# Context rows of the pooling layer normed while the down projection runs, and the layer's first panel read for context rows first

## The chip, the core and the metric

The kernel runs on one core of a Trainium2 chip. Five engines work side by side and meet only in semaphores: TensorE (PE, with its weight loads as PEld), VectorE (DVE), ScalarE (ACT), GpSimd (POOL) and SyncE (SP), which issues most of the DMAs. The metric is the device time of one execution in microseconds, the median of several runs; lower is better.

## The reference, cut to what matters

The program is two transformer blocks in a row on 256 tokens ("latent" rows) of width 2048. The first ends in a gated feed-forward layer; the second starts with a pooling layer that works on the latent rows and, apart from them, on 256 "context" rows with weights in common. Both sets of rows are normed, scaled and shifted before the pooling layer's input projection:

```python
x = x + jnp.einsum('bsf,fd->bsd', jax.nn.silu(gate) * up, w_down[l])      # 5632 -> 2048
...
shift, scale, gate = jnp.split(jax.nn.silu(c) @ ada_w[i] + ada_b[i], 3, axis=-1)
h_lat = rms_norm(x, pre_norm[i]) * (1 + scale[:, None]) + shift[:, None]
shift_c, scale_c, gate_c = jnp.split(jax.nn.silu(c_ctx) @ ada_w[i] + ada_b[i], 3, axis=-1)
h_ctx = rms_norm(ctx, pre_norm[i]) * (1 + scale_c) + shift_c
# pool_branch(h), for h_lat and h_ctx:
u, gate = jnp.split(h @ w_in, 2, axis=-1)
p = centred_multiscale_pool(u.reshape(B, L, POOL_GROUPS, POOL_GROUP_DIM))
```

h_lat needs x after the last column of the down projection. h_ctx needs nothing of the first block: only the input ctx, and the vectors shift and scale (the "ada" products), which the kernel computes on VectorE along the way.

## The kernel before, in words

**Weights as a stream of chunks.** All weight matrices pass through one ring of four slots (RING). A chunk is 256 rows by 512 columns, 512 KB. SP loads it into `raw`; ACT rounds it to `hi` (L541); DVE writes `lo` = raw - hi (L545); PE multiplies with both, three products for each (L598, `by_tokens`), since the fp32 values are carried as a high and a low part. SP may load the next chunk into a slot when `lo` of the old one is written (`lo_split`); ACT may overwrite `hi` when PE has used the old one (`chunks_used`). Between the weight chunks come chunks of the ada matrix, which PE does not see: DVE multiplies them with a vector in four instructions (L574). The order of both kinds is a list written out in advance (`DOWN_ORDER`, `POOL_ORDER`), and each engine has its own program in which the calls `his`, `los` and `by_tokens` walk through that list; whatever else stands between two calls runs at that place of its engine and holds back what is behind it.

**The down projection.** Four panels of 512 output columns, 22 weight chunks each, in two turns (i = 0 and 1) of two panels. In a turn the weight chunks are called w0 to w43 here; w22 is the first of the second panel. Twelve matmuls (2 of rows by 2 of tokens by 3) make a chunk. Eight ada chunks (a0 to a7, a8 to a15) lie among the chunks of each panel; in the second half the stream reads w31 w32 a12 w33 w34 a13 w35 w36 w37 a14 w38 w39 a15 w40 w41 w42 w43. After each panel DVE adds the sums in PSUM to the residual (`add_panel`, L1621) and ACT squares the new columns (`panel_squares`, L682).

**From there to the pooling layer.** `n_pool` is one norm over four token tiles, in two parts: context rows first, then latent rows. The context part is done near the end of turn 1: ACT squares its rows (L673), DVE forms the mean (L749), POOL the root (L754), DVE scales the rows (L759). The latent part follows the last `add_panel`. When both are scaled PE turns the rows to columns (transposes, L775) in 16 groups of four, four groups ahead of the first chunk and four more ahead of each of the next three; ACT applies scale and shift from PSUM to `shift_tmp` (L805), DVE writes `h_hi` (L830) and `h_lo` (L837) out of it. Four banks of PSUM hold the turned groups, so group g waits for `h_lo` of group g - 4. Each chunk of the first pooling panel (L598 again, 24 matmuls, four token tiles) waits for the norm's groups that it reads. The averaging matrix `poolm` (1 MB), first read at L2202, is loaded by a DMA that ACT issues (L1299) after the last `add_panel`, and PE waits for it ahead of the transposes. The tiles `h4_hi` and `h4_lo` lie over the tiles `g_hi` and `g_lo`, which the down projection reads to its last chunk.

## Time and profile before

| | us |
|---|---|
| median of 3 runs | 2441.76 |
| lowest and highest | 2439.11 and 2446.45 |
| the profiled execution's own time | 2439.29 |
| its span in the trace | 2437.5 |
| mean granted TensorE clock | 0.987 of full |

```profile
PE 2336.4 (96%) x11221; PEld 1935.8 (79%) x11221; DVE 1656.9 (68%) x2401; ACT 1041.2 (43%) x1490; POOL 76.2 (3%) x112
PE   8999999999999999999969999999999699899997
PEclk9999999999999999999989999999999899999999
```

The first line gives each engine's busy time, its share of the span and its instructions. The other two cut the span into 40 slices of 61 us, each digit a tenth: how busy PE was, and which share of full speed its clock was granted. PE is the engine that is busy nearly all the time, save in a few slices; the digit 6 in the 21st slice (1219 to 1280 us) is the passage from the down projection to the pooling layer.

### The profile page before, as it was taken

The numbers are of one execution on the slowest core, as the hardware profiler recorded it, in microseconds if no ns is written. First come the engines' busy times: TensorE is split into PE (matmuls) and PEld (weight loads), VectorE is DVE, ScalarE is ACT, GpSimd is POOL, SyncE is SP. The second block draws the span as 40 slices with busy tenths as digits, with TensorE's granted clock in tenths as the row PEclk, the third lists the DMA queues.
The fourth block names the chain that finished last, engine by engine and source line by source line (L and its number), as shares of the span: only waits on it lengthen the run. The fifth ranks groups of instructions, "written<-read, shape, count | busy, mean of one in ns | idle before, by whom it ended". The sixth has DMA issues, their size and how long they took to land.

```text
span 2437.5 us, 32050 instructions
## 1 busy us (share of the span) xinstructions
PE 2336.4 (96%) x11221; PEld 1935.8 (79%) x11221; DVE 1656.9 (68%) x2401; ACT 1041.2 (43%) x1490; POOL 76.2 (3%) x112
## 2 busy tenths in 40 slices
PE   8999999999999999999969999999999699899997
PEld 6778778878877877778858888887788699799976
DVE  5378866687787786777748585756758666456544
ACT  5575654555555555333342222222222535443433
POOL 1022210000000000000000000000000000000000
PEclk9999999999999999999989999999999899999999
DMA  7956545666676766777735464645557256312243
GB/s 240 206 167 197 165 137 158 189 217 219 209 234 199 232 212 201 249 238 243 249 108 185 144 198 137 200 139 171 205 169 221 82 170 181 114 61 68 74 140 136
DMA packets 225516, 430.32 MB, mean 177 GB/s; under 512 B 13800, under 2 KB 38624, under 8 KB 224129
## 3 DMA queue, kind: packets, MB, share of 16 engines
q1 hardware_dynamic: 222112, 418.96, 55.2%
q10 hardware_dynamic: 2720, 9.83, 1.3%
q8 instruction: 63, 1.03, 0.2%
q14 instruction: 45, 0.36, 0.1%
q0 software_dynamic: 576, 0.14, 0.0%
HBM read 426.16 MB, written 2.72 MB: 176 GB/s over the span
## 4 chain that ended last, share of the span: by engine, by line
PE 63%; issue 19%; DVE 7%; DMA 6%; ACT 4%; DVEq 0%; POOL 0%; ACTq 0%; SPq 0%; POOLq 0%
PE ps L598 37%; PE ps L631 11%; PE ps L608 9%; DMA raw<-in_w_down 4%; DVE lo L545 2%; ACT hi L541 2%; DVE ada_acc L574 2%; PE ps L647 1%; DVE ustage L1630 1%; DMA raw<-in_w_in 1%; PE ps L2202 1%; PE ps L2127 0%; DMA poolm<-const_pool 0%; PE ps L1979 0%; PE ps L775 0%
## 5 line engine op out<-in xcount | busy, mean ns | idle before, releaser
L541 ACT ACTIVATE hi<-raw 128x1024 fp32r<-128x1024 f32 x604 | 635.3, 1059 | 1148.8 <-PE ps L598 536.2
L545 DVE TENSOR_TENSOR lo<-raw,hi 128x1024 fp32r<-128x1024 f32 x604 | 731.4, 1222 | 520.4 <-ACT hi L541 517.5
L574 DVE SCALAR_TENSOR_TENSOR ada_acc<-raw,csil,ada_acc 128x512 f32<-128x512 f32 x720 | 491.8, 746 | 2.5 <-DMA raw<-in_ada_w 2.3
L598 PE MATMUL ps<-hi,h_hi 128*128 128x512 f32 x960 | 383.2, 399 | 8.1 <-DVE lo L545 6.5
L598 PE MATMUL ps<-hi,h_lo 128*128 128x512 f32 x960 | 378.9, 395 | 0.0
L598 PE MATMUL ps<-lo,h_hi 128*128 128x512 f32 x960 | 378.7, 395 | 0.0
L598 PEld LDWEIGHTS ps<-hi,h_hi 128*128 128x128 f32 x960 | 180.8, 188 | 55.4 <-DVE lo L545 13.4
L598 PEld LDWEIGHTS ps<-hi,h_lo 128*128 128x128 f32 x960 | 180.7, 188 | 42.5
L598 PEld LDWEIGHTS ps<-lo,h_hi 128*128 128x128 f32 x960 | 180.9, 188 | 40.1
L598 PE MATMUL ps<-hi,g_hi 128*128 128x512 f32 x352 | 140.9, 400 | 6.6 <-DVE lo L545 6.3
L631 PE MATMUL ps<-hi,h_hi 128*128 128x512 f32 (+1 forms) x352 | 142.2, 404 | 2.9 <-DVE h_lo L736 2.9
L598 PE MATMUL ps<-lo,g_hi 128*128 128x512 f32 x352 | 139.1, 395 | 0.0
L598 PE MATMUL ps<-hi,g_lo 128*128 128x512 f32 x352 | 139.0, 395 | 0.0
L631 PE MATMUL ps<-hi,h_lo 128*128 128x512 f32 (+1 forms) x352 | 136.9, 389 | 0.0
L631 PE MATMUL ps<-lo,h_hi 128*128 128x512 f32 (+1 forms) x352 | 136.6, 388 | 0.0
L598 PE MATMUL ps<-hi,k_hi 128*128 128x448 f32 (+2 forms) x288 | 102.6, 356 | 1.1 <-DVE k_lo L837 0.6
L598 PE MATMUL ps<-hi,y_hi 128*128 128x512 f32 x256 | 102.6, 401 | 0.0
L608 PE MATMUL ps<-h_hi,hi 128*128 128x512 f32 x256 | 102.0, 398 | 0.0
L598 PE MATMUL ps<-hi,y_lo 128*128 128x512 f32 x256 | 101.9, 398 | 0.0
L598 PE MATMUL ps<-lo,y_hi 128*128 128x512 f32 x256 | 101.9, 398 | 0.0
L598 PE MATMUL ps<-hi,k_lo 128*128 128x448 f32 (+2 forms) x288 | 101.5, 353 | 0.0
L598 PE MATMUL ps<-lo,k_hi 128*128 128x448 f32 (+2 forms) x288 | 101.5, 352 | 0.0
(320 smaller groups left out, 3710.3 us busy)
## 6 DMA issues: line engine op xcount, KB each, us to landing
raw<-in_ada_w SPq DMA_DIRECT2D x192, 512.0 KB, 4.2
raw<-in_w_up SPq DMA_DIRECT2D x176, 512.0 KB, 4.5
raw<-in_w_down SPq DMA_DIRECT2D x88, 512.0 KB, 5.4
raw<-in_w_in SPq DMA_DIRECT2D x84, 512.0 KB, 4.5
raw<-in_pool_w_in SPq DMA_DIRECT2D x64, 512.0 KB, 4.1
raw<-in_mla_w_in SPq DMA_DIRECT2D x56, 448.0 KB, 4.1
raw<-in_w_out SPq DMA_DIRECT2D x32, 512.0 KB, 3.8
raw<-in_pool_w_out SPq DMA_DIRECT2D x32, 512.0 KB, 4.7
```

What stands on the lines that cost most here:

```text
L541: act.activation(hi[:, slot, :, :], raw[:, slot, :, :], ACT.Copy).then_inc(hi_split, 1 + ada)
L545: dve.tensor_tensor(lo[:, slot, :, :], raw[:, slot, :, :], hi[:, slot, :, :].bitcast(F32), ALU.subtract).then_inc(lo_split, 1)
L574: ins = dve.scalar_tensor_tensor(acc, raw[:, slot, k, :], csil[:, v, kt:kt + 1], acc, ALU.mult, ALU.add)
L598: mm = pe.matmul(ps[:, bank, 0:n], a[:, kt0 + k, tok * P:(tok + 1) * P], w[:, slot, k, col0:col0 + n], start=first and k == 0 and s == 0, ...
L608: mm = pe.matmul(ps[:, bank0 + n, :], w[:, slot, k, n * P:(n + 1) * P], a[:, kt0 + k, :], start=first and k == 0 and s == 0, stop=last and ...
L631: mm = pe.matmul(ps[:, PAIR * half + tok, 0:width], x, w[:, k, :], start=first and k == 0 and s == 0, stop=last and k == nk - 1 and s == 2)
L647: mm = pe.matmul(ps[:, bank, at:at + 1], acc, negones[:, 0:1], start=True, stop=True)
L1630: ins = dve.scalar_tensor_tensor(conv[which][:, m, back:SEQ], turned_u(m)[:, 0:SEQ - back], cols[:, bass.ds(ch + vec[0] * P + vec[1], 1)], ...
L2202: mm = pe.matmul(ps[:, m, s * SEQ + c0:(s + 1) * SEQ], u[:, TT * s + k, m * P:(m + 1) * P], poolm[:, bass.ds(n, 1), k, c0:].rearrange("p a ...
```

## The change

Nine edits, all around that passage.

1. `n_pool` is split in two norms of two token tiles, `n_pool_ctx` and `n_pool` (latent), of eight groups each; a group is still four transposes. `g_hi` and `g_lo` become halves of one tile that interleaves them, so that both free the same low addresses as the down projection goes on, and `h4_hi` and `h4_lo` of the context rows can be written while it runs.
2. The context rows are squared (ACT), their mean formed and the rows scaled (DVE) in turn 0 of the down projection, between its chunks.
3. In the second panel of turn 1, ahead of each of the chunks w31 to w38, PE makes one group of context transposes (`ctx_turn`, into banks 4 and 7 by turns); ACT writes both the shifted rows and `h_hi` from PSUM, four activations for a group (`ctx_high`); DVE writes `h_lo` (`ctx_low`).
4. The two panels of a turn swap their banks of PSUM, so that the last one leaves the banks of the context tiles free.
5. The scales and shifts are made (`scales`) at the start of turn 1.
6. The DMA of `poolm` is issued in turn 0, and PE waits for it only at its first use.
7. At the end DVE adds the last panel ahead of the third of the next stage's `lo` instead of behind it.
8. PE's loop over the two turns is written out.
9. The first pooling panel (`first_pool_panel`) takes its first four chunks for the context tiles, then the same four, which are kept in the ring (`frees=False`), for the latent tiles, then the last four for both.

```diff
+CTX_FROM = FT // CK_T + CH + 1
...
-        g_hi = pl("g_hi", [P, FT, SEQ], F32R)
-        g_lo = pl("g_lo", [P, FT, SEQ], F32R)
+        g = pl("g", [P, FT, 2, SEQ], F32R)
+        g_hi, g_lo = g[:, :, 0, :], g[:, :, 1, :]
...
+        def ctx_turn(pe, g):
+            n = n_pool_ctx
+            if g == 0:
+                pe.wait_ge(n.scaled, n.scaled0 + n.nt)
+            else:
+                pe.wait_ge(n.hi_done, n.groups0 + max(g - 1, 0))
...
+        def ctx_high(act, g):
+            n = n_pool_ctx
+            act.wait_ge(n.turned, n.groups0 + g + 1)
...
+            for to, done in (((lambda m: n.tmp[:, g % SHIFT_BUFS, m * SEQ:(m + 1) * SEQ]), n.shifted),
+                             ((lambda m: n.hi[:, g * n.per + m, :]), n.hi_done)):
+                for m in range(n.per):
...
+        def ctx_low(dve, g):
+            n = n_pool_ctx
+            dve.wait_ge(n.shifted, n.groups_shifted0 + g + 1)
+            dve.wait_ge(n.hi_done, n.groups0 + g + 1)
+            dve.tensor_tensor(n.lo[:, g * n.per:(g + 1) * n.per, :],
...
         @block.scalar
-                if i == D // W // 2 - 1:
-                    norm_squares(act, n_pool, lambda e, i: e.wait_ge(ctx_loaded, 16), 0, xn4[:, 0, :])
+                if last:
+                    act.wait_ge(scales_ready, 2)
+                    for g in range(n_pool_ctx.groups):
+                        end = place(DOWN_ORDER, CTX_FROM + g) + RING
+                        his(act, C_DOWN, i, step, at, end)
+                        ctx_high(act, g)
+                        at = end
+                else:
+                    act.wait_ge(g_lo_done, FREE + N_UP)
+                    act.dma_start(poolm[:, :, :, :], consts["pool"]).then_inc(poolm_loaded, 16)
+                    end = place(DOWN_ORDER, CTX_FROM) + RING
+                    his(act, C_DOWN, i, step, at, end)
+                    norm_squares(act, n_pool_ctx, lambda e, i: e.wait_ge(ctx_loaded, 16), 0, xn4[:, 0, :])
...
         @block.tensor
-            pe.wait_ge(poolm_loaded, 16)
+            def first_pool_panel():
+                part = lambda s, j, frees: by_tokens(pe, C_POOL + j, (C_POOL + j) % RING, h4_hi, h4_lo, CK_T * j, streams[s * TT:(s + 1) * TT],
+                                                     W, j == 0, False, ada_behind(C_POOL + j), frees)
+                pe.wait_ge(ffn_added, PAIR + D // W - 1)
+                pe.wait_ge(n_pool_ctx.lo_done, n_pool_ctx.all_groups)
+                for j in range(RING):
+                    if j == RING - 1:
+                        pe.wait_ge(ffn_added, PAIR + D // W)
+                        pe.wait_ge(ada_taken, FREE + ADA_POOL)
+                        norm_turn(pe, n_pool, 0, TURN_BANKS)
+                    part(CTX, j, False)
+                for j in range(RING):
+                    if j:
+                        norm_turn(pe, n_pool, TURN_BANKS + 2 * (j - 1), min(TURN_BANKS + 2 * j, n_pool.groups))
+                    pe.wait_ge(n_pool.lo_done, n_pool.groups0 + j + 1)
+                    part(LAT, j, True)
```

The instruction streams show three places. First ACT in the second panel of turn 1, around chunk w34 (`hi` is the weight chunk's high part, `xn` the norm's rows, `h_hi` the normed columns). Before:

```order
L541 ACTIVATE hi<-raw 128x1024 [waits chunks_used,raw_loaded0]
L541 ACTIVATE hi<-raw 128x1024 [waits chunks_used,raw_loaded2]
L541 ACTIVATE hi<-raw 128x1024 [waits chunks_used,raw_loaded3]
L541 ACTIVATE hi<-raw 128x1024 [waits chunks_used,raw_loaded1]
L541 ACTIVATE hi<-raw 128x1024 [waits chunks_used,raw_loaded2]
```

The second, third and fourth of these in the changed kernel:

```order
L543 ACTIVATE hi<-raw 128x1024 [waits chunks_used,raw_loaded2]
L815 ACTIVATE ctx_tmp<-ps,adat,hscale 128x256 [waits norm_turned]
L815 ACTIVATE ctx_tmp<-ps,adat,hscale 128x256
L815 ACTIVATE h_hi<-ps,adat,hscale 128x256 x2
L543 ACTIVATE hi<-raw 128x1024 [waits chunks_used,raw_loaded3]
L815 ACTIVATE ctx_tmp<-ps,adat,hscale 128x256 [waits norm_turned]
L815 ACTIVATE ctx_tmp<-ps,adat,hscale 128x256
L815 ACTIVATE h_hi<-ps,adat,hscale 128x256 x2
L543 ACTIVATE hi<-raw 128x1024 [waits chunks_used,raw_loaded1]
```

Four activations now stand between one chunk's `hi` and the next, eight times over. The second place is DVE at the end of the down projection. Before:

```order
L749 TENSOR_SCALAR ms<-ss 128x2 [waits norm_squared]
L759 TENSOR_SCALAR xn_112<-xn_112,rstd 128x2048 [waits norm_root]
L759 TENSOR_SCALAR xn_112<-xn_112,rstd 128x2048
L545 TENSOR_TENSOR lo<-raw,hi 128x1024 [waits hi_split] x3
L653 TENSOR_SCALAR adat<-ps 128x8 [waits ada_turned]
L1621 TENSOR_TENSOR xres<-ps,xres 128x2x512 [waits chunks_used]
```

And now:

```order
L824 TENSOR_TENSOR h_lo<-ctx_tmp,h_hi 128x2x256 [waits norm_hi_done,norm_shifted]
L547 TENSOR_TENSOR lo<-raw,hi 128x1024 [waits hi_split] x5
L656 TENSOR_SCALAR adat<-ps 128x8 [waits ada_turned]
L1674 TENSOR_TENSOR xres<-ps,xres 128x2x512 [waits chunks_used]
L547 TENSOR_TENSOR lo<-raw,hi 128x1024 [waits hi_split]
L748 TENSOR_REDUCE ss<-panel_sums 128x2 [waits x_squared]
```

The context norm is gone from ahead of the last addition to the residual, and one `lo` has moved behind it. The third place is the same norm on DVE where it has gone, turn 0 of the down projection, between the chunks w36 and w37:

```order
L576 SCALAR_TENSOR_TENSOR ada_acc<-raw,csil,ada_acc 128x512 [waits ada_added] x2
L547 TENSOR_TENSOR lo<-raw,hi 128x1024 [waits hi_split] x2
L752 TENSOR_SCALAR ms<-ss 128x2 [waits norm_squared]
L762 TENSOR_SCALAR xn_111<-xn_111,rstd 128x2048 [waits norm_root]
L762 TENSOR_SCALAR xn_111<-xn_111,rstd 128x2048
L547 TENSOR_TENSOR lo<-raw,hi 128x1024 [waits hi_split]
```

What stood here before was three `lo` in a row, behind the same ada chunk.

## Rows read from the trace of the kernel before

**Rows 1.** Windows: length, busy us (count) of PE, PEld, DVE, ACT, POOL; clock, DMA share, GB/s.
```profile
1172.00:1235.00 63.00, 61.66 (x280) 49.60 (x278) 45.88 (x53) 28.37 (x31) 0.69 (x1) 1.00 0.75 238
1235.00:1253.70 18.70, 3.68 (x17) 3.28 (x17) 10.76 (x19) 6.12 (x13) 0.70 (x1) 0.63 0.49 168
```

**Rows 2.** Waits, 985 to 1262 us: who waited for whom, us, times, longest.
```profile
ACT hi L541 <- DMA raw<-in_w_down: 127.4, 67, 5.4
PE ps L775 <- DMA poolm<-const_pool: 13.7, 1, 13.7
PE ps L598 <- DVE lo L545: 6.3, 10, 0.9
```

**Rows 3.** Timeline of PE, end of down projection to pooling panel: start, us, what, [idle].
```profile
1231.73 0.48 PE L598 MATMUL ps<-hi,g_hi 128*128 128x512 f32 x1
...
1234.38 0.40 PE L598 MATMUL ps<-hi,g_lo 128*128 128x512 f32 x1
1248.50 3.68 PE L775 MATMUL ps<-ident,xn 128*128 128x128 f32 x16 [13.73 <-DMA poolm<-const_pool]
1253.70 0.51 PE L598 MATMUL ps<-hi,h_hi 128*128 128x512 f32 x1 [1.52 <-DVE h_lo L837]
...
1259.38 1.47 PE L775 MATMUL ps<-ident,xn 128*128 128x128 f32 x12
...
1262.56 0.48 PE L598 MATMUL ps<-hi,h_hi 128*128 128x512 f32 x1
...
1308.35 0.40 PE L608 MATMUL ps<-h_hi,hi 128*128 128x512 f32 x1
```

**Rows 4.** Timeline of DVE in the same stretch.
```profile
1231.90 2.48 DVE L759 TENSOR_SCALAR xn<-xn,rstd 128x2048 f32<-128x2048 f32 x2 [0.81 <-POOL rstd L754]
1234.30 3.49 DVE L545 TENSOR_TENSOR lo<-raw,hi 128x1024 fp32r<-128x1024 f32 x3
...
1237.78 1.22 DVE L1621 TENSOR_TENSOR xres<-ps,xres 128x1024 f32<-128x1024 f32 x1
...
1241.71 2.48 DVE L759 TENSOR_SCALAR xn<-xres,rstd 128x2048 f32<-128x2048 f32 x2 [0.81 <-POOL rstd L754]
...
1261.41 0.68 DVE L837 TENSOR_TENSOR h_lo<-shift_tmp,h_hi 128x512 fp32r<-128x512 f32 x1
1262.01 0.42 DVE L830 CAST h_hi<-shift_tmp 128x512 fp32r<-128x512 f32 x1
```

**Rows 5.** Timeline of ACT in the same stretch.
```profile
1226.81 1.90 ACT L673 ACTIVATE xn<-xn 128x2048 f32<-128x2048 f32 x1
...
1230.80 2.94 ACT L541 ACTIVATE hi<-raw 128x1024 fp32r<-128x1024 f32 x3
...
1260.02 3.85 ACT L805 ACTIVATE shift_tmp<-ps,adat,hscale 128x256 f32<-128x256 f32 x8 [6.55 <-PE ps L775]
```

**Rows 6.** DMA issues, 975 to 1000 us: count, size, us to landing.
```profile
raw<-in_ada_w SPq DMA_DIRECT2D x3, 512.0 KB, 6.1
```

**Rows 7.** DMA issues, 985 to 1236 us.
```profile
raw<-in_ada_w SPq DMA_DIRECT2D x30, 512.0 KB, 4.8
```

**Rows 8.** Timelines of ACT, DVE and PE in turn 0, chunks w33 to w37.
```profile
1071.40 1.06 ACT L541 ACTIVATE hi<-raw 128x1024 fp32r<-128x1024 f32 x1 [0.31 <-DMA raw<-in_w_down]
...
1080.46 1.06 ACT L541 ACTIVATE hi<-raw 128x1024 fp32r<-128x1024 f32 x1 [0.27 <-DMA raw<-in_w_down]
1071.12 2.59 DVE L545 TENSOR_TENSOR lo<-raw,hi 128x1024 fp32r<-128x1024 f32 x2 [0.44 <-ACT hi L541]
1073.63 2.73 DVE L574 SCALAR_TENSOR_TENSOR ada_acc<-raw,csil,ada_acc 128x512 f32<-128x512 f32 x4
...
1078.88 0.50 PE L598 MATMUL ps<-hi,g_hi 128*128 128x512 f32 x1 [0.62 <-DVE lo L545]
```

**Rows 9.** Groups by line, 1193.5 to 1226 us: count, busy us, mean ns, idle before.
```profile
L545 DVE TENSOR_TENSOR lo<-raw,hi 128x1024 fp32r<-128x1024 f32 x12 | 14.7, 1225 | 6.8 <-ACT hi L541 6.6
L541 ACT ACTIVATE hi<-raw 128x1024 fp32r<-128x1024 f32 x12 | 12.7, 1061 | 21.6 <-DMA raw<-in_w_down 21.6
```

More of the change, by code:

```diff
@@ L589, in los, with by_tokens @@
                     split_lo(dve, i * step + c, c % RING)
-        def by_tokens(pe, c, slot, a_hi, a_lo, kt0, outs, width, first, last, ada=0):
+        def by_tokens(pe, c, slot, a_hi, a_lo, kt0, outs, width, first, last, ada=0, frees=True):
             pe.wait_ge(lo_split, c + RING + 1)
@@ L599, in by_tokens @@
                                        start=first and k == 0 and s == 0, stop=last and k == CK_T - 1 and s == 2)
-            mm.then_inc(chunks_used, 1 + ada)
+            if frees:
+                mm.then_inc(chunks_used, 1 + ada)
         def by_channels(pe, c, slot, a_hi, a_lo, kt0, bank0, first, last, ada=0):
@@ L787, in norm_ahead @@
                 pe.wait_ge(n.lo_done, n.groups0 + -(-(j + 1) * CK_T // n.per))
+        def ctx_turn(pe, g):
[5 more added lines that the diff above has]
+            for m in range(n.per):
+                for i in range(n.nt):
+                    mm = pe.transpose(ps[:, 4 + 3 * (g % 2), (m * n.nt + i) * P:(m * n.nt + i + 1) * P],
+                                      n.xn(i)[:, (g * n.per + m) * P:(g * n.per + m + 1) * P], ident)
+            mm.then_inc(n.turned, 1)
+        def ctx_high(act, g):
+            n = n_pool_ctx
+            act.wait_ge(n.turned, n.groups0 + g + 1)
+            if g >= SHIFT_BUFS:
+                act.wait_ge(n.lo_done, n.groups0 + g - SHIFT_BUFS + 1)
+            for to, done in (((lambda m: n.tmp[:, g % SHIFT_BUFS, m * SEQ:(m + 1) * SEQ]), n.shifted),
+                             ((lambda m: n.hi[:, g * n.per + m, :]), n.hi_done)):
+                for m in range(n.per):
+                    k = g * n.per + m
+                    ins = act.activation(to(m), ps[:, 4 + 3 * (g % 2), m * SEQ:(m + 1) * SEQ], ACT.Identity,
+                                         scale=n.scale(k, 0), bias=n.shift(k, 0))
+                ins.then_inc(done, 1)
+        def ctx_low(dve, g):
[3 more added lines that the diff above has]
+            dve.tensor_tensor(n.lo[:, g * n.per:(g + 1) * n.per, :],
+                              n.tmp[:, g % SHIFT_BUFS, :].rearrange("p (m n) -> p m n", m=n.per),
+                              n.hi[:, g * n.per:(g + 1) * n.per, :].bitcast(F32), ALU.subtract).then_inc(n.lo_done, 1)
         def norm_parts(n, g):
@@ L1080, in _ @@
             x_power(pool, 1)
-            for part in range(2):
-                norm_root(pool, n_pool, part)
+            norm_root(pool, n_pool_ctx)
+            norm_root(pool, n_pool)
             def yout_roots(m):
@@ L1620, in add_panel @@
                 v = xres[:, :, bass.ds(col0, W)]
-                dve.tensor_tensor(v, ps[:, 2 * half:2 * half + 2, :], v, ALU.add).then_inc(done, 1)
+                dve.tensor_tensor(v, ps[:, 2 - 2 * half:4 - 2 * half, :], v, ALU.add).then_inc(done, 1)
             def older_taps(i, which):
@@ L1723, in yout_join @@
                    .then_inc(yout_added[m], 1)
-            scales(0, V_PRE0)
-            norm_mean(dve, n_pool, 1)
-            norm_apply(dve, n_pool, 1)
+            n = FT // CK_T
+            for i in range(D // W // 2):
+                order, step, last = DOWN_ORDER, len(DOWN_ORDER), i == D // W // 2 - 1
+                mid = place(order, DOWN_TURN) + 1 + RING
+                end = place(order, n) + RING
+                split = lambda a, b: los(dve, C_DOWN, i, step, a, b, ADA_DOWN, 2)
+                if last:
+                    scales(0, V_PRE0)
+                split(RING, end)
+                add_panel(ffn_added, i * step + used(C_DOWN + end - RING), 0, i * 2 * W)
+                split(end, mid)
+                take_ada(dve, i * 2 + ADA_DOWN, 5)
+                at = mid
+                if last:
+                    for g in range(n_pool_ctx.groups):
+                        to = place(order, CTX_FROM + g) + RING
+                        split(at, to)
+                        ctx_low(dve, g)
+                        at = to
+                else:
+                    to = place(order, CTX_FROM + 3) + RING
+                    split(at, to)
+                    norm_mean(dve, n_pool_ctx)
+                    norm_apply(dve, n_pool_ctx)
+                    at = to
+                split(at, step)
+                los(dve, C_DOWN, i, step, step, step + RING - 1 - int(last))
+                take_ada(dve, i * 2 + ADA_DOWN + 1, 5)
+                add_panel(ffn_added, i * step + used(C_DOWN + step), 1, i * 2 * W + W)
+                los(dve, C_DOWN, i, step, step + RING - 1 - int(last), step + RING - int(last))
+            norm_mean(dve, n_pool)
+            norm_apply(dve, n_pool)
+            los(dve, C_DOWN, D // W // 2 - 1, step, step + RING - 1, step + RING)
             norm_shift_split(dve, n_pool)
@@ L2164, in _ @@
             n = FT // CK_T
-            with pe.Fori(0, D // W // 2) as i:
+            for i in range(D // W // 2):
                 def ada_before(j):
+                    if i == D // W // 2 - 1 and 0 <= j - CTX_FROM < n_pool_ctx.groups:
+                        ctx_turn(pe, j - CTX_FROM)
                     if j < n and j * CK_T % 4 == 0:
```

56 lines of the change are left out of this document (26 added, 30 removed).

## The prediction

> **What bounds the kernel now.** I read the windows first, then the waits, then the timelines of the engines in two stretches. In the windows the reader is to see a down projection in which PE is busy 61.7 of 63.0 us, and then 18.7 us in which it is busy 3.7, on a clock granted at 0.63, between its two levels of 1.2 and 2.4 GHz [rows 1]. The waits name two things. In the passage, PE stands 13.7 us for the DMA of `poolm`. In the down projection ACT stands 127.4 us for weight chunks still being loaded, and PE ten times, 6.3 us together, for `lo` [rows 2]. So PE is the bound there by a small margin, and the ring behind it (load, `hi`, `lo`, free the slot, load again) is nearly as slow: little can be put into ACT or DVE without PE seeing it.
>
> **The passage, before.** The last down chunk, w43, starts on PE at 1231.73 and its last matmul at 1234.38; the first pooling panel starts at 1253.70, and the instruction behind that panel (L608) at 1308.35 [rows 3]. From the start of w43 to L608: 76.62 us. In it, 24 matmuls of a pooling chunk take 5.58 us at the steady pace (0.2325 us each; 1253.70 to 1259.38 with the start), eight chunks 44.64 us, and w43 2.79 us. The remaining 29.2 us are a gap of 19.2 us (1234.5 to 1253.70) and three breaks of about 3.3 us: from the transposes at 1259.38 to the next matmul at 1262.56 it is 3.18 us [rows 3]. The gap has layers. DVE adds the last columns at 1237.78, though PE was done 3 us before, since the context norm and three `lo` stood ahead; the latent rows are scaled at 1244.2 [rows 4]; then only `poolm` is missing, until 1248.5. So `poolm` alone is worth 4.3 us, not the 13.7 of its row.
>
> **The passage, after.** Call T the time at which w43 is done. At T PE can go on with context tiles, 12 matmuls or 2.79 us for each of four chunks. Meanwhile the chain to the latent rows runs: from the start of the addition to scaled rows it takes 1237.78 to 1244.19, 6.4 us, with work between that is now elsewhere [rows 4]. It is done at T+6.7, and PE asks for it ahead of the fourth chunk, at T+8.4: 1.7 us to spare. There it makes 16 transposes. Twelve take 1.47 us in a row, 0.102 each without the tail [rows 3], so 16 and the restart of the matmuls take 1.72 us. ACT starts 0.64 us after the first group (1260.02 against 1259.38) and needs 0.48 us for an activation, 0.96 for a group [rows 3, 5]; on DVE a group takes a cast and a subtraction, 0.94 us (0.60 from subtraction to cast, 0.34 for the cast) [rows 4]. With the cast of group 1 ahead of `h_lo` of group 0, that `h_lo` is done at T+12.1. PE ends the fourth context chunk at 8.4 + 1.7 + 2.8 = T+12.9. The latent halves follow at T+12.9, 16.6, 20.3 and 23.1, with eight transposes (0.91 us) ahead of the second and third; each finds its group ready. The next chunk's `hi` waits on ACT for the last of the eight groups (T+22.0), its `lo` is done at T+24.9, and PE wants it at T+25.9. Behind it stand two ada chunks (4.9 us), then the next `lo` at T+30.8, wanted at T+31.4. The margins are 1.7, 0.8, 1.0 and 0.6 us, and I count no wait. From w43's start to L608: 2.79 + 44.64 + 1.72 + 2 x 0.91 = 51.0 us. **Saved: 76.6 - 51.0 = 25.6 us.** If the margins fail one after another, up to 4 us of it go.
>
> **Turn 0 pays for the context norm.** ACT's squares take from 1226.81 to 1230.80, 4.0 us [rows 5]. They now stand ahead of `hi` of w34, which starts at 1071.40 right behind its load [rows 8]: it starts at 1075.0 instead, its `lo` is done at 1077.4 instead of 1073.7, and PE, which took w34 at 1075.3, takes it 2.1 us late. The ada chunk behind (2.65 us) then pushes `lo` of w35 to 1081.2 against 1078.88, when PE took it with no slack [rows 8]: 2.3 us late. DVE's part, 0.17 + 0.81 idle for POOL + 2.48 [rows 4], ends at 1085.8; w37, whose load is later too (it was split at 1080.46 [rows 8], and its slot frees 3.7 us late), is done at 1087.0: 2.4 us late, so this part is nearly hidden. But the ada chunks and `lo` of w38 to w40 stand behind it, and their slots free 3.5 to 4.3 us late: PE takes w38 3.5 us late and w40 4.2 us. After that PE was ahead of the ring no longer than its own pace allows, and nothing is caught up. **+4.2 us.** Bounds: 2 us (later slack takes some back) and 4.0 + 3.5 = 7.5 us, both blocks in full.
>
> The DMA of `poolm` lands in the ring's busiest stretch. The trace has a like case: while the 2 MB of context rows were loaded, ada chunks took 6.1 us to land, against 4.8 in the whole stage [rows 6, 7]: 1.3 us. For 1 MB and a ring of which every load counts I take **+1 us**, between 0 and 3. The Trainium skill, "DMA: Bandwidth & Descriptors", section "Issuing engines are not separate DMA queues", says that transfers issued by different engines share the same 16 DMA engines and interleave, so ACT's queue gives no way round the ring. By that rule all of 1 MB would come out of the ring's bandwidth, an estimate of 3 us at the 238 GB/s and 0.75 busy of [rows 1], and the sum would be 2 us worse; the trace's 1.3 us for twice the bytes speaks for less.
>
> **Turn 1 pays for the context groups.** Eight times four transposes cost PE 0.41 us and 0.09 at the restart, 4.0 us in all, and give the ring that much more time. ACT gets 8 x 1.93 us. It was idle 21.6 us over 12 `hi` in this stretch, 1.8 each, and DVE 6.8 us [rows 9]. `ctx_low` is 0.60 us [rows 4], in the time in which DVE waits for `hi` anyway. Walking through w33 to w43 as above, with three ada chunks between: `lo` of w35 at 1208.6 for PE at 1208.55, w38 at 1217.5 for 1218.5, w40 at 1224.2 for 1224.1, w41 at 1227.0 for 1227.0. So ACT and DVE are just full, PE just not held up, and the two short waits that it had before here (0.56 and 0.55 us, among the ten) are swallowed. w43 starts 2.6 us later than before. **+2.6 us.** This is an operation of which the trace has no copy: ACT writes the rounded high part straight from PSUM with scale and bias. Its nearest row is the 0.48 us of L805 [rows 5]. Bounds: 1 us, and 4.0 + 8 x (1.93 - 1.8 / 2) = 12 us if half the idle time of ACT is not where it is wanted.
>
> The rest I take at nothing: PE's loop written out (w43 of turn 0 to w0 of turn 1 was 2.88 us from start to start, 0.09 over the pace), the scales in turn 1 (0.5 us on DVE, where PE was 3 to 4 us behind the ring), the swap of banks, the interleaved tile (the same elements for each instruction).
>
> **The sum.** -25.6 + 4.2 + 1.0 + 2.6 = -17.8 us. Against the profiled execution's 2439.3 us it is 2421.5; that execution lay 2.5 us under the median of the runs, which would give 2424. I forecast 2423.
>
> **The rivals.**
> *The ring pays little* (chance 0.12). What is late in turn 0 is caught up, `poolm` is free: costs 3 us instead of 7.8, 2418. For it: PE was 3 to 4 us behind the ring at the end of turn 0. Against: that slack is used up by w4 of turn 1, and the ring is late by as much.
> *The panel's start is not ready* (0.10). The four margins of 0.6 to 1.7 us fail, or the first pooling chunks' `lo`, now behind the eight `ctx_low`, come late: 5 us back, 2428. Against: the raw chunks are there, and only two `lo` are left ahead of T.
> *The ring pays about double* (0.15). The two walks assume that landing times move only by what their slots are late. If each ACT block falls where a load has just landed, turn 1 costs 8 and turn 0 7.5 with 2 for the DMA: 17.5 against 25.6, 2433.
> *The ring pays for everything: slower* (0.05). One mechanism: a ring of four slots bound by latency has no free time, and each microsecond given to ACT or DVE in it returns on PE. Price: turn 0 4.0 + 3.5 + 3, turn 1 8 x (1.93 + 0.60) = 20.2: 30.7 us, 5 more than the passage gives, 2446. It decides once the insertions cost over 25.6 us. For it: ACT's 127.4 us of waits are all for loads. Against: they are idle time of ACT, 1.8 us each, which the insertions fill.
> *The change doesn't do what it says* (0.03): a wait serialises context tiles and norm as before, and only the 7 us of `poolm` and the late addition are won against 7.8 paid: no change, 2441.
>
> **How the numbers follow.** My forecast has 0.55. Differences under 0.3%, 7 us, can't be told from no change. Faster by more: the forecast, the cheap ring, the late start and most of the double price, 0.88. Within: the rest of the double price and the last rival, 0.07. Slower 0.05. The forecast's own range is 2418 to 2428; with the neighbours to both sides 2414 to 2433, which leaves the slower cases and a part of the double price out.
>
> **What would show it.** Right: L608 starts about 51 us after w43; no idle PE over 2 us between w43 and L608, and a granted clock of 1.00 there; w43 of turn 1 starts 6 to 10 us later than 1231.73; in turn 1 PE waits for `lo` within w31 to w43 sum to under 2 us; `poolm` is no releaser of PE. Wrong: idle time of PE ahead of the transposes or between the latent halves (the start); PE's waits for `lo` in the two second halves over 15 us (the ring).

## The result: 2420.05 us, a ratio of 0.992

The changed kernel took 2420.05 us (median of 4 runs, 2417.38 to 2424.76) against 2440.44 us of the kernel before on the same chip: ratio 0.992, 95% interval 0.9899 to 0.9941. A second comparison gave 2418.37 against 2437.94 us, 0.992 (0.9906 to 0.9933). The forecast was 2423.

The profiled execution took 2424.76 us, its span is 2423.0 us. From its page:

```profile
PE 2336.9 (96%) x11221; PEld 1935.5 (80%) x11221; DVE 1652.8 (68%) x2393; ACT 1048.0 (43%) x1506; POOL 75.1 (3%) x112
PE   8999999999999999999999999998999699899997
PEclk9999999999999999999999999999999899899999
```

TensorE does the same work in the same busy time; its digit 6 in the 21st slice has become a 9. Where the 14.5 us between the two spans are, by the starts of the same matmuls on TensorE (w0 of turn 0, w0 of turn 1, w43 of turn 1, L608, which is L611 here):

| | before | after | difference |
|---|---|---|---|
| to w0 of turn 0 | 971.58 | 977.95 | +6.37 |
| turn 0 | 135.04 | 137.35 | +2.31 |
| turn 1 to w43 | 125.11 | 127.86 | +2.75 |
| passage, w43 to L608 | 76.62 | 51.01 | -25.61 |
| from there to the end | 1129.14 | 1128.78 | -0.36 |

Nothing was put into or taken out of the first row; only the layout of `g_hi` and `g_lo`, which are written there, is new. In the thirteen other executions profiled for this document it lies between 968.8 and 976.0 us, with a mean of 973.0 us over the three kernels with the old layout and 972.8 us over the eleven executions with the new one: it is scatter, and it hides 6 us of the gain in this pair of profiles, though not in the medians.

**The passage.** Windows of the changed kernel (columns as in [rows 1]), its waits (994 to 1270 us), and TensorE's timeline, which answer to [rows 1 to 3]:

```profile
1181.00:1243.16 62.16, 61.94 (x299) 50.22 (x298) 49.63 (x59) 38.48 (x58) 0.00 (x0) 1.00 0.74 244
1243.16:1265.00 21.84, 21.84 (x109) 18.14 (x109) 11.37 (x19) 8.09 (x17) 0.70 (x1) 1.00 0.24 75
```

```profile
ACT hi L543 <- DMA raw<-in_w_down: 108.7, 52, 5.9
...
PE ps L600 <- DVE lo L547: 6.9, 9, 1.9
```

```profile
1243.16 0.48 PE L600 MATMUL ps<-hi,g 128*128 128x512 f32 x1
...
1246.04 0.39 PE L600 MATMUL ps<-hi,h_hi 128*128 128x512 f32 x1
...
1254.41 1.91 PE L778 MATMUL ps<-ident,xn 128*128 128x128 f32 x16
1256.07 0.48 PE L600 MATMUL ps<-hi,h_hi 128*128 128x512 f32 x1
...
1261.73 1.03 PE L778 MATMUL ps<-ident,xn 128*128 128x128 f32 x8
...
1265.40 1.03 PE L778 MATMUL ps<-ident,xn 128*128 128x128 f32 x8
...
1271.85 0.39 PE L600 MATMUL ps<-hi,h_hi 128*128 128x512 f32 x1
...
1277.43 0.40 PE L600 MATMUL ps<-hi,h_hi 128*128 128x512 f32 x1
...
1294.17 0.40 PE L611 MATMUL ps<-h_hi,hi 128*128 128x512 f32 x1
```

Where there were 13.7 and 1.5 us of idle time [rows 3], no row has a bracket: TensorE is busy 21.84 of 21.84 us, at a clock of 1.00 instead of 0.63. The context matmuls (`h_hi` at 1246.04) begin 0.23 us behind the last one of w43, the pace of any two matmuls. With T = 1245.95 (w43's start and 2.79) the transposes are at T+8.46 and the fourth context chunk at T+10.12. The latent halves follow at T+13.0, 16.6, 20.2 and 23.1, the second and third behind eight transposes each (1261.73 and 1265.40); the fifth chunk, for all four tiles, is at T+25.9 (1271.85), the sixth at T+31.5 (1277.43), and L611 is 51.01 us behind the start of w43. `poolm` releases nobody.

The latent chain beside it, on DVE and ACT, for [rows 4, 5]:

```profile
1246.24 1.23 DVE L1674 TENSOR_TENSOR xres<-ps,xres 128x1024 f32<-128x1024 f32 x1 [2.74 <-PE ps L600]
...
1250.19 2.48 DVE L762 TENSOR_SCALAR xn<-xres,rstd 128x2048 f32<-128x2048 f32 x2 [0.81 <-POOL rstd L757]
```

```profile
1257.35 0.68 DVE L876 TENSOR_TENSOR h_lo<-shift_tmp,h_hi 128x512 fp32r<-128x512 f32 x1
...
1269.57 1.22 DVE L547 TENSOR_TENSOR lo<-raw,hi 128x1024 fp32r<-128x1024 f32 x1
...
1275.48 1.22 DVE L547 TENSOR_TENSOR lo<-raw,hi 128x1024 fp32r<-128x1024 f32 x1
```

```profile
1255.04 3.76 ACT L844 ACTIVATE shift_tmp<-ps,adat,hscale 128x256 f32<-128x256 f32 x8 [5.11 <-PE ps L778]
```

The rows are scaled when DVE's next instruction starts, 1252.59 or T+6.6, 1.8 us before TensorE asks. The other three margins can be read from the same rows. The first `h_lo` is done at 1258.03 and the first latent half starts at 1258.95: 0.9 us. `lo` of the fifth chunk is done at 1270.79 for 1271.85: 1.1 us. `lo` of the sixth is done at 1276.70 for 1277.43: 0.7 us.

**The turns.** In turn 1, among the context groups, grouped by line (for [rows 9]):

```profile
L547 DVE TENSOR_TENSOR lo<-raw,hi 128x1024 fp32r<-128x1024 f32 x11 | 13.4, 1221 | 1.9 <-ACT hi L543 1.9
L543 ACT ACTIVATE hi<-raw 128x1024 fp32r<-128x1024 f32 x12 | 12.9, 1077 | 9.4 <-DMA raw<-in_w_down 8.4 <-PE ps L600 1.0
...
L815 ACT ACTIVATE h_hi<-ps,adat,hscale 128x256 fp32r<-128x256 f32 x16 | 8.4, 601 | 0.0
L815 ACT ACTIVATE ctx_tmp<-ps,adat,hscale 128x256 f32<-128x256 f32 x16 | 8.3, 588 | 0.0
```

ACT's idle time ahead of 12 `hi` went from 21.6 to 9.4 us: the groups' activations lie in it. TensorE waits for `lo` only once between w31 and w43, 0.22 us. Both new forms (0.60 and 0.59 us alone, about 0.50 each in a row of four) cost what L805 costs. In turn 0, around w34, on ACT and on TensorE (for [rows 8]):

```profile
1076.01 1.06 ACT L543 ACTIVATE hi<-raw 128x1024 fp32r<-128x1024 f32 x1 [4.91 <-DMA raw<-in_w_down]
1076.97 1.90 ACT L676 ACTIVATE xn<-xn 128x2048 f32<-128x2048 f32 x1
...
1080.96 3.17 ACT L543 ACTIVATE hi<-raw 128x1024 fp32r<-128x1024 f32 x3
1087.64 1.06 ACT L543 ACTIVATE hi<-raw 128x1024 fp32r<-128x1024 f32 x1 [3.50 <-DMA raw<-in_w_down]
```

```profile
1083.32 0.50 PE L600 MATMUL ps<-hi,g 128*128 128x512 f32 x1 [1.87 <-DVE lo L547]
...
1087.10 0.50 PE L600 MATMUL ps<-hi,g 128*128 128x512 f32 x1 [0.72 <-DVE lo L547]
```

The squares take ACT's 4.0 us ahead of w34 and TensorE waits 1.87 us for its `lo`; counted from w31, w34 starts 2.0 us later than before, near the 2.1 predicted. (In the mean of nine executions it is only 0.9 us.) ACT then rounds three chunks in a row, and soon it waits 3.5 us for a load again: it has caught up.

### The profile page after: what moved, and what is told of

Read it like the earlier page. It is cut to its first block, busy times and chain, and to the rows that moved or that the text cites. A ratio compares the mean times of both kernels' runs of the same rounds, so it can differ in the third digit from the quotient of the medians.

```text
span 2423.0 us, 31984 instructions
## 1 busy us (share of the span) xinstructions
PE 2336.9 (96%) x11221; PEld 1935.5 (80%) x11221; DVE 1652.8 (68%) x2393; ACT 1048.0 (43%) x1506; POOL 75.1 (3%) x112
## 4 chain that ended last, share of the span: by engine, by line
PE 64%; issue 19%; DVE 7%; DMA 5%; ACT 4%; DVEq 0%; POOL 0%; SPq 0%; ACTq 0%; POOLq 0%
PE ps L600 38%; PE ps L634 11%; PE ps L611 9%; DMA raw<-in_w_down 3%; DVE lo L547 2%; ACT hi L543 2%; DVE ada_acc L576 2%; PE ps L650 1%; DVE ustage L1683 1%; DMA raw<-in_w_in 1%; PE ps L2295 1%; DMA xres<-in_x 1%; PE ps L2193 0%; PE ps L2045 0%; PE ps L2044 0%
## 5 line engine op out<-in xcount | busy, mean ns | idle before, releaser
L600 PE MATMUL ps<-hi,g 128*128 128x512 f32 x704 | 227.8, 400 | 7.0 <-DVE lo L547 6.9
L600 PEld LDWEIGHTS ps<-hi,g 128*128 128x128 f32 x704 | 133.2, 189 | 43.0 <-DVE lo L547 12.0
L600 PE MATMUL ps<-lo,g 128*128 128x512 f32 x352 | 139.3, 396 | 0.0
L611 PE MATMUL ps<-h_hi,hi 128*128 128x512 f32 x256 | 102.0, 398 | 0.0
```

The lines of the kernel that those rows point to most:

```text
L600: mm = pe.matmul(ps[:, bank, 0:n], a[:, kt0 + k, tok * P:(tok + 1) * P], w[:, slot, k, col0:col0 + n], start=first and k == 0 and s == 0, ...
L611: mm = pe.matmul(ps[:, bank0 + n, :], w[:, slot, k, n * P:(n + 1) * P], a[:, kt0 + k, :], start=first and k == 0 and s == 0, stop=last and ...
```

## The experiments

All times are in us. "Turn 1" is to w43. The columns before the median are of the one profiled execution. The ratio is to the kernel before in the same comparison, whose medians there lay between 2437.94 and 2440.44, so medians from different comparisons are not compared directly.

| kernel | turn 0 | turn 1 | passage | median | ratio to before (95%) |
|---|---|---|---|---|---|
| before | 135.04 | 125.11 | 76.62 | 2440.44 | |
| changed | 137.35 | 127.86 | 51.01 | 2420.05 | 0.992 (0.9899-0.9941) |
| changed, again | 134.91 | 128.09 | 50.97 | 2418.37 | 0.992 (0.9906-0.9933) |
| poolm_wait_only | 132.87 | 127.18 | 73.21 | 2436.72 | 0.9983 (0.997-0.9996) |
| poolm_early_only | 134.14 | 124.92 | 71.39 | 2436.18 | 0.999 (0.9977-1.0002) |
| poolm_late | 135.55 | 127.15 | 51.00 | 2414.78 | 0.99 (0.9877-0.9924) |
| poolm_late, again | 137.43 | 128.18 | 50.97 | 2418.10 | 0.9918 (0.9904-0.9931) |
| norm_at_turn_end | 136.24 | 129.53 | 50.97 | 2415.24 | 0.9904 (0.9886-0.9923) |
| both_moves | 132.06 | 130.11 | 50.99 | 2414.15 | 0.99 (0.9882-0.9917) |
| act_fuller | 133.59 | 145.57 | 50.97 | 2435.07 | 0.9985 (0.9974-0.9997) |
| chain_late | 137.37 | 128.85 | 51.02 | 2419.47 | 0.9912 (0.9893-0.993) |
| chain_later | 134.51 | 127.15 | 52.67 | 2416.43 | 0.9917 (0.9902-0.9932) |
| whole_chunks | 134.02 | 127.99 | 62.53 | 2428.67 | 0.9962 (0.9952-0.9972) |
| whole_chunks_busy | 136.47 | 127.32 | 59.79 | 2427.03 | 0.9956 (0.994-0.9971) |

The passage repeats to 0.05 us, since nothing in it waits for the ring. The turns scatter by 2 us and more between executions with the same code, so their cost is read from means.

**poolm_wait_only and poolm_early_only: the averaging matrix alone.** Both edit the kernel before. The first moves only the wait, the second the issue too:

```diff
# poolm_wait_only, block of TensorE
-            pe.wait_ge(poolm_loaded, 16)
...
+                if n == 0:
+                    pe.wait_ge(poolm_loaded, 16)      # ahead of the first matmul with poolm
# poolm_early_only, in addition, block of ACT
+                if i == 0:
+                    act.wait_ge(g_lo_done, FREE + N_UP)
+                    act.dma_start(poolm[:, :, :, :], consts["pool"]).then_inc(poolm_loaded, 16)
-            act.wait_ge(ffn_added, PAIR + D // W)
-            act.dma_start(poolm[:, :, :, :], consts["pool"]).then_inc(poolm_loaded, 16)
```

> The kernel before with one edit: PE waits for the averaging matrix at its first use and no longer ahead of the transposes; its DMA stays where it was. Theory (what ends last in the passage are the latent rows, scaled 4.3 us before the matrix lands): w43 to the by-channels matmuls falls from 76.6 to 72.3 us, the kernel 4.3 us (0.18%) faster. Rival (the matrix was the wait, as its 13.7 us in the table of waits say): the passage falls by 8 us or more.

> The kernel before with two edits: the same, and the DMA of the matrix issued in turn 0 of the down projection. Theory: the passage 72.3 us as with the wait moved alone, and turn 0 of the down projection (135.0 us from w0 to w0) about 1 us longer, since 1 MB goes through the DMA engines that feed the ring; kernel 3.3 us faster. Rival (the whole megabyte comes out of the ring's bandwidth): turn 0 is 3 us longer or more. Second rival (it is free): under 0.3 us.

TensorE in poolm_early_only, where the row of 13.7 us stood:

```profile
1243.12 3.60 PE L775 MATMUL ps<-ident,xn 128*128 128x128 f32 x16 [8.64 <-DVE xn L759]
1248.29 0.50 PE L598 MATMUL ps<-hi,h_hi 128*128 128x512 f32 x1 [1.57 <-DVE h_lo L837]
```

The wait of 13.7 us for `poolm` became one of 8.6 us for the scaled rows: the passage is 71.39 us, 5.2 shorter, not 13.7 (3.4 shorter with the wait alone; there a part of the first chunk ran at the lower clock). The 4.3 us expected lie between the two. Of the medians, only that of poolm_wait_only is clear of the kernel before; the interval of poolm_early_only takes in 1. A releaser's row is worth only what it stands above the next one. The other 20.4 us of the passage need the other edits; whole_chunks, below, divides them.

**poolm_late, and again: does its DMA cost the ring?**

```diff
                 else:
-                    act.wait_ge(g_lo_done, FREE + N_UP)
-                    act.dma_start(poolm[:, :, :, :], consts["pool"]).then_inc(poolm_loaded, 16)
...
+            act.dma_start(poolm[:, :, :, :], consts["pool"]).then_inc(poolm_loaded, 16)
             norm_hi(act, n_pool)
```

> The changed kernel with the matrix's DMA issued where it was before, at the end of the down projection (PE still waits for it only at first use). Theory: turn 0 loses its 1 us, so 136.3 us instead of 137.35; the passage stays at 51.0 us, since nothing of the first pooling panel needs the matrix and the DMA has 48 us; kernel within 1 us of the changed one. Rival (a DMA there delays the pooling chunks, whose margins are 0.6 to 1.0 us): passage 52 to 54 us.

> The changed kernel with the DMA of the averaging matrix behind the last rounding of turn 1, once more, on the same chip as the changed kernel. If 1 MB in turn 0's ring costs something (prediction: 1 us, the rule on shared DMA engines: 3 us): that much under the changed kernel of this comparison. If not: the same within 1 us.

> The changed kernel once more. The time that its first profile showed for turn 0 (137.35 us) was 1.7 to 5.3 us over that of three variants with the same code in that turn (133.6 to 136.2). If that was scatter between executions: turn 0 between 133.5 and 136.5 us, and a median within 2 us of the variants with both costs moved (2414 to 2415). If not: 137 us and 2420.

The first comparison gave 2414.8, 5 us under the changed kernel's first. The passage stayed at 51.0 us, as expected. On one chip in one comparison they gave 2418.10 and 2418.37: no difference. Nor do the traces show one: turn 0 with the norm took 133.6 to 137.4 us in the seven executions with the DMA in it (mean 135.5), 135.6 and 137.4 in the two without. The 5 us were scatter. after_again was right in turn 0 (134.91 us) and wrong in the median, which was to be within 2 us of 2414 to 2415. The DMA does share the engines: landing takes 7.0 us amid the ring,

```profile
poolm<-const_pool ACTq DMA_DIRECT2D x1, 1024.0 KB, 7.0
```

against 5.0 us in poolm_late (6.9 to 8.5 us in the nine executions that issue it in turn 0, 4.8 to 5.0 in the three that issue it behind the last rounding of turn 1). TensorE seems to feel it too, a few chunks later. In the changed kernel it stops ahead of w29:

```profile
1066.27 0.50 PE L600 MATMUL ps<-hi,g 128*128 128x512 f32 x1 [0.87 <-DVE lo L547]
```

In five of the nine executions with the DMA in turn 0, TensorE stops for 0.9 to 1.2 us (by the starts) ahead of w28 or w29, and in none of the five without it. From w24 to w31 the means are 23.2 us with it and 22.6 without, with ranges that overlap (22.6 to 23.7, and 21.8 to 23.3). So a cost of about half a microsecond there is likely but not shown, and it can't be found again in the whole turn.

**norm_at_turn_end and both_moves: does it matter where the context norm stands?** Squares, mean and scaling go to the end of turn 0; both_moves has poolm_late's edit as well.

```diff
# ACT: squares ahead of the last rounding of turn 0
+                his(act, C_DOWN, i, step, at, RING + step - 1)
+                if not last:
                     norm_squares(act, n_pool_ctx, ...)
+                    his(act, C_DOWN, i, step, RING + step - 1, RING + step)
# DVE
                 add_panel(ffn_added, i * step + used(C_DOWN + step), 1, i * 2 * W + W)
+                if not last:
+                    norm_mean(dve, n_pool_ctx)
                 los(dve, C_DOWN, i, step, step + RING - 1 - int(last), step + RING - int(last))
+                if not last:
+                    norm_apply(dve, n_pool_ctx)
```

> The changed kernel, but the context norm of turn 0 is taken at that turn's end: its squares on ACT ahead of the last rounding of the turn, its mean and scaling on DVE behind the addition of the panel. My first theory (each microsecond in the second half of a turn comes back on TensorE) puts the norm at 4 us there and expects turn 0 plus turn 1 to be 2 to 3 us shorter than in the changed kernel, where they are 137.35 and 127.86 us. The rival from the runs so far (the norm costs 1.7 us wherever it stands) expects no more than 1 us either way. The passage stays at 51.0 us by both.

> The changed kernel with the context norm at the end of turn 0 and the DMA of the averaging matrix behind the last rounding of turn 1. If the two costs are apart and real: 3 us under the changed kernel. If what was measured of them so far is the scatter between executions: within 1.5 us of it. The passage stays at 51.0 us.

Turn 0 and turn 1 together took 265.8 and 262.2 us. The eight executions with the norm in its place (all with the context groups, without act_fuller) took 261.7 to 266.2, mean 263.8: no effect of the place can be seen, and two executions could not show one under 2 us. The first theory of norm_at_turn_end, 2 to 3 us less than 265.2, did not come true. That of both_moves, 3 us less, did by the number, but after_again took 263.0 us with nothing moved. Turn 1 is longer with the norm at the end of turn 0 (129.5 and 130.1 us against a mean of 127.8), so the cost seems to move with it. Neither kernel is measurably faster than the changed one: the intervals of their ratios overlap those of after_again and poolm_late_again.

**act_fuller: is ACT full?**

```diff
             act.wait_ge(n.turned, n.groups0 + g + 1)
...
+            for r in range(4):
+                if g or r:
+                    act.wait_ge(spared, 4 * g + r)
+                act.activation(spare[:, :], ps[:, 4 + 3 * (g % 2), 0:SEQ], ACT.Identity, ...).then_inc(spared, 1)
```

> The changed kernel with four spare activations (PSUM to a tile that nobody reads, 0.48 us each or a little more) ahead of each of the eight context groups in turn 1. The output is the same. The prediction's theory (with the context groups ACT is just full, 1.8 us of idle time for each rounding against 1.93 us put in): each further 2 us on ACT comes back on TensorE, turn 1 to w43 goes from 127.9 to 140 us or more, L611 up to 12 to 15 us later, about 2433. The rival (the ring has slack that the walk did not see, since loads run ahead): under 4 us, about 2424.

Its groups, waits and window between 1200 and 1255 us:

```profile
L815 ACT ACTIVATE spare<-ps,adat,hscale 128x256 f32<-128x256 f32 x32 | 18.2, 568 | 0.8
```

```profile
PE ps L802 <- ACT h_hi L821: 8.7, 5, 2.4
...
PE ps L601 <- DVE lo L548: 3.4, 1, 3.4
```

```profile
1200.00:1255.00 55.00, 42.90 (x191) 33.29 (x189) 32.74 (x38) 45.63 (x78) 0.00 (x0) 0.94 0.56 180
```

Turn 1 became 17.7 us longer for 18.2 us of spare work: nearly all came back, half of it as TensorE's direct wait for a group's `h_hi` ahead of the next group; ACT is busy 45.6 of 55 us here, and the gaps cost TensorE some of its clock too (0.94). That shows that ACT had no room for twice the activations, not that it had none at all. While the groups last, ACT runs without a stop, 5.0 us for a group and a rounding, of which 2.3 are spare; the 2.75 us that remain are less than the 3.23 us that TensorE needs for a chunk and its transposes (1.79 of each 2.3 us came back there, most of the rest behind the last group, in the wait of 3.4 us and at the lower clock). How much less than 2.3 us a group would have gone in free was not tried.

**chain_late and chain_later: how thin is the margin of the latent rows?** Two spare additions on DVE ahead of the mean, then three behind the root:

```diff
# chain_late
+            for s in range(2):
+                dve.tensor_tensor(spare[:, s, :], xn4[:, TT, 0:1024], xn4[:, TT, 1024:2048], ALU.add)
             norm_mean(dve, n_pool)
# chain_later
             norm_mean(dve, n_pool)
+            dve.wait_ge(n_pool.root, n_pool.means0 + 1)
+            for s in range(3):
+                dve.tensor_tensor(xn4[:, TT + s // 2, ...], xres[:, 0, 0:1024], xres[:, 0, 1024:2048], ALU.add)
             norm_apply(dve, n_pool)
```

> The changed kernel with two spare additions of 128x1024 on DVE (1.2 us each, 2.4 together) between the last addition to the residual and the mean of the latent rows. The output is the same. By the prediction's margins (latent rows scaled at T+6.7, asked for at T+8.4) TensorE waits 0.7 us ahead of the transposes and nothing more: passage 51.7 us. If the chain to the latent rows is on the path all the same: 53.4. If the margins behind it (0.6 to 1.0 us, for the groups and the next chunk's low part) are thinner than worked out: over 52.5, with waits of TensorE between the latent halves.

> The changed kernel with three spare additions of 128x1024 on DVE (1.17 us each, 3.5 together) behind the root of the latent norm and ahead of the scaling of its rows, where nothing of the chain can hide them. The output is the same. In the changed kernel the latent rows are scaled at T+6.64 and TensorE turns them at T+8.46 without waiting. Theory (a margin of 1.8 us, and nothing else of the chain within 1 us of being late): scaled at T+10.15, TensorE idle 1.7 us ahead of the transposes, passage 52.7 us, all else as before. Rival (the groups or the next low part have thinner margins): over 53.5 us, with waits of TensorE between the latent halves.

chain_late decided little: a part of the additions fell into DVE's wait for ACT's squares, the rows were scaled at T+8.4, and TensorE asked at that moment (passage 51.02). In chain_later nothing hid them:

```profile
1243.76 0.30 PE L778 MATMUL ps<-ident,xn 128*128 128x128 f32 x1 [0.45 <-DVE xn L762]
1244.86 1.86 PE L778 MATMUL ps<-ident,xn 128*128 128x128 f32 x15 [0.81 <-DVE xn L762]
1246.48 0.48 PE L600 MATMUL ps<-hi,h_hi 128*128 128x512 f32 x1
```

The rows are scaled at T+10.0, 3.4 us later than in the changed kernel. TensorE stands 1.3 us by the brackets (1.7 us in starts), nowhere else, and the passage is 52.67 us for 52.7 expected. The margin is 1.7 to 1.8 us, and what follows moves along with TensorE.

**whole_chunks and whole_chunks_busy: what the split of chunks is worth.** The first undoes edit 9 alone: after w43 the panel waits for the latent rows and takes each chunk for all four tiles. The second adds 24 spare matmuls into that wait:

```diff
                 pe.wait_ge(n_pool_ctx.lo_done, n_pool_ctx.all_groups)
+                pe.wait_ge(lo_split, C_POOL + RING + 1)                       # busy only
+                for _ in range(24):                                           # busy only
+                    pe.matmul(ps[:, 4, 0:W], h4_hi[:, 0, SEQ:SEQ + P], hi[:, C_POOL % RING, 0, 0:W], start=True, stop=True)
+                pe.wait_ge(ffn_added, PAIR + D // W)
+                pe.wait_ge(ada_taken, FREE + ADA_POOL)
                 for j in range(RING):
...
-                    part(CTX, j, False)
+                    norm_turn(pe, n_pool, TURN_BANKS + 2 * (j - 1) if j else 0, min(TURN_BANKS + 2 * j, n_pool.groups))
+                    pe.wait_ge(n_pool.lo_done, n_pool.groups0 + j + 1)
+                    by_tokens(pe, C_POOL + j, ..., CK_T * j, streams, W, j == 0, False, ada_behind(C_POOL + j))
```

> The changed kernel with the first pooling panel taken in whole chunks: PE waits for the latent rows ahead of the first chunk, then takes each chunk for all four token tiles. Theory (the halves fill the latent chain): the latent rows are scaled at T+6.7, the first h_lo is there at T+10.4, and the matmuls start there instead of at T; later chunks find their groups ready. Passage 51.0 + 10.4 - 1.7 = 59.7 us, kernel 8.7 us slower than the changed one, still 11 to 12 us faster than before. Rival (early norm and early matrix are what gave the gain, the halves little): passage under 54 us. Other rival (the two breaks of 3.3 us return too): over 63 us.

> The kernel with whole chunks in the first panel (whole_chunks), but with 24 spare matmuls of 128x512 (a bank of PSUM that nobody reads; 5.6 us at 0.2325 us each) on TensorE between the last down chunk and the latent rows. The output is the same. If the passage of 62.5 us there was 59.7 plus a clock at half speed after 5.8 us without work: no matmul of the first chunk at 0.43 us, passage 59.7 to 60.2 us. If the slow matmuls have another cause (the restart behind the transposes, weights just written): 62.5 us again.

TensorE in whole_chunks, and its windows behind the gap:

```profile
1242.14 0.45 PE L778 MATMUL ps<-ident,xn 128*128 128x128 f32 x1 [5.41 <-DVE xn L762]
1243.24 3.46 PE L778 MATMUL ps<-ident,xn 128*128 128x128 f32 x15 [0.66 <-DVE xn L762]
1247.23 0.79 PE L600 MATMUL ps<-hi,h_hi 128*128 128x512 f32 x1 [0.53 <-DVE h_lo L876]
```

```profile
1242.10:1247.20 5.10, 3.91 (x16) 3.25 (x16) 3.70 (x6) 3.02 (x7) 0.00 (x0) 0.50 0.34 104
1247.20:1252.60 5.40, 5.37 (x13) 4.21 (x14) 1.85 (x4) 0.74 (x2) 0.00 (x0) 0.50 0.02 6
1252.60:1258.00 5.40, 5.40 (x29) 4.53 (x28) 0.91 (x2) 1.94 (x4) 0.00 (x0) 0.99 0.01 3
```

And the same place in whole_chunks_busy:

```profile
1237.94 5.74 PE L2255 MATMUL ps<-hi,h_hi 128*128 128x512 f32 x24
...
1244.62 1.86 PE L778 MATMUL ps<-ident,xn 128*128 128x128 f32 x15 [0.81 <-DVE xn L762]
1248.26 0.50 PE L600 MATMUL ps<-hi,h_hi 128*128 128x512 f32 x1 [1.77 <-DVE h_lo L876]
```

The expectation for whole_chunks missed by 2.8 us: the mechanism was as expected, but behind 5.4 us without work the clock stood at 0.50, its level of 1.2 GHz, for ten microseconds more, through the transposes and 12 matmuls behind them, which had only that pace (0.43 us from start to start for 0.23). With useless matmuls in the gap the clock stayed at 1.00, the first real matmul came 0.36 us sooner, and the passage was 59.79 us, in the expected range. So of the 11.5 us that whole_chunks' passage is longer than the changed kernel's, 8.8 are the latent chain, behind which no other work is left to do, and 2.7 the clock. The ratios of the two to the kernel before, 0.9962 and 0.9956, do not tell them apart.

With poolm_early_only this divides the 25.6 us. `poolm` gave 5.2 (76.62 to 71.39). The context rows made ready early gave 8.9 (71.39 to 62.53), with no change in the order of the panel: the gap behind w43 fell from 14.0 to 10.8 us and three breaks of 3.3 us became two of 0.9, though the slow matmuls took some of it back. The order of the panel gave 11.5 (62.53 to 51.01).

## Why the prediction was right, and which terms were not

**What bounds the kernel.** Right. The passage gave all of the gain, and the ring took some back; act_fuller shows how close the ring is.

**The passage: -25.6 us.** Measured -25.61: 51.01 us for 51.0. The transposes came at T+8.46 for T+8.4, and the latent halves at T+13.0, 16.6, 20.2 and 23.1 for 12.9, 16.6, 20.3 and 23.1. The four margins held: 1.8, 0.9, 1.1 and 0.7 us in the trace for 1.7, 0.8, 1.0 and 0.6. The first is bracketed by two runs: 1.8 us of delay cost nothing, 3.4 us cost 1.7. The other three were not tested by delays of their own. The layers of the gap were right too: `poolm` alone was put at 4.3 us, and its removal gave 5.2 and 3.4.

**Turn 0: the context norm, +4.2 us. This term was mis-sized.** Turn 0 took 135.7 us in the mean of nine executions with the norm in it (133.6 to 137.4), 134.0 in the mean of three without (132.9 to 135.0): +1.7, with a spread of each execution as large as that. From w31 to the end of the turn the scatter is smaller: 41.4 to 43.5 us in the nine, 40.2 to 40.7 in the three, +1.8. Counted from w31, the means of the starts are 0.9 us late at w34, 1.3 at w35, 2.2 at w38 and 1.8 from w40 on, where the walk had 2.1, 2.3, 3.5 and 4.2. From w34 to w38 it was nearly right (1.3 us added for 1.4). Two steps failed, by 1.2 and 1.1 us. The one is w34 itself, "2.1 us late": TensorE's own wait ahead of w33, 0.9 us in the mean of the three, is 0.3 us in the mean of the nine, and w34 follows w33 1.5 us later than it did, not 2.1. Why the wait ahead of w33 is shorter stays open. It is not the squares: w33 stands ahead of them, and norm_at_turn_end and both_moves, which have none there, wait 0.5 and 0.3 us. The other is from w38 to w40, "nothing is caught up": the walk added 0.7 us there, and 0.4 to 0.5 us were caught up instead. Kernels without the norm wait there of themselves, 0.5 us in the mean ahead of w40, and with the norm this wait is gone: the lateness swallowed it. I had reckoned with that in turn 1, and not in turn 0.

**`poolm` in the ring: +1.0 us.** Turn 0 is no longer with the DMA in it than without, but with a scatter of 2 us an execution 1 us could hide, and the waits ahead of w28 and w29 speak for about half of it. Of this term the size stays open. The Trainium skill, "DMA: Bandwidth & Descriptors", section "Issuing engines are not separate DMA queues", says that the copies share the engines and interleave. The trace agrees for the copy itself (7.0 us to land against 5.0 in poolm_late). That all of its bytes would be missing from the ring, which was my reading of it, no run here shows.

**Turn 1: the context groups, +2.6 us.** Mean 127.8 us of eight executions against 125.7 of three: +2.1. From w30 to w42, where the groups stand, it is +2.8, with ranges that do not touch (37.0 to 38.2 us against 34.1 to 35.2). The parts are a little other than laid out: a group costs TensorE 0.44 us and not 0.50, 3.5 in all; 0.5 us of waits remain, and 1.2 us of waits that the kernels before had are gone. Up to w30 the turn is 0.7 us shorter in the mean, which is within the scatter of the three (85.4 to 87.9 us). That ACT is "just full" was only shown in part: act_fuller shows that there is no room for as much again.

**The sum.** -25.6 + 1.7 + 2.1 = -21.8 us against -17.8 predicted; the medians differ by 20.4 and 19.6. On the profiled execution the forecast was 2421.5 us, and 2424.8 came: that one began its down projection 6.4 us later than the one before, by scatter. The same scatter spoils one of the signs given: w43 of turn 1 was to start 6 to 10 us later than 1231.73 and started 11.4 us later, 6.4 of them from ahead of the down projection and only 5.1 from the two turns. The other signs of being right came as written.

**The rivals.** The nearest is *The ring pays little* (3 us, 2418): the cost measured, 3.8 us, lies nearer to its 3 than to my 7.8, and its reason against, that a late ring stays late, is in part the one that failed. The medians, 2420.05 and 2418.37, lie between its 2418 and my 2423 and nearer to it; that they are within the forecast's range of 2418 to 2428 does not speak for my two terms of turn 0. *The panel's start is not ready*, *The ring pays about double* and *The ring pays for everything* are out; act_fuller's 17.7 us show that the last one's mechanism is real with twice the activations in each group.

## What to carry to other kernels

Order a stage's inputs by when they are ready, and start on those that are: work that TensorE has to do anyway is a good filler of a dependency's latency, and here it kept the clock at 1.00 where 5.4 us of idle time brought it to 0.50. The longest wait in a profile is worth only its distance to the next releaser behind it; here 13.7 us were 5. When something is put into a loop that is nearly bound by its ring, walk the lateness chunk by chunk but take off the waits that the loop had already, and measure how full the filler engine is: here 18.2 us more on ACT cost 17.7.

## What the runs showed of the hardware beyond that

- The clock behind a gap differs with no pattern that these runs settle. Behind 5.4 us of idle time the transposes and 12 matmuls ran at the lower level. Behind 8.9 us (poolm_wait_only) the transposes took 3.3 us, the clock was back at 1.00 and four matmuls had full pace; then it fell again, 1.0 us behind a second stop of 1.9 us, and seven matmuls ran at the lower level. Behind 8.6 us (poolm_early_only) and 13.7 us (before) the transposes took 3.6 and 3.7 us instead of 1.9, but the matmuls behind them had full pace.
- The same code does not take the same time: the part ahead of the down projection varied by 9 us over fourteen profiled executions, a turn of it by 4 us, while the passage, which waits for no load, repeated to 0.05 us. Two medians of one kernel from different comparisons (poolm_late) were 3.3 us apart. A gain of 2 us has to be read from a stretch whose start and end are near it, as w31 to the end of the turn, and not from medians.
